# Hybrid HGRN2 / RWKV-7 / MoE trunk on one core: two branch phases joined, two gate units and 13 dense products per pair at other places

## The reference, cut to what matters

```python
xn = rmsnorm(h, norm_mix_w)
z = xn @ w_in                                   # 2048 x 11552
zq, zf, zi, zo, zs, zga, zgb = split(z)         # 4 x 1024 | 3360 | 2048 | 2048
y_hg = hgrn2_branch(zq, zf, zi, zo, lb, onorm_w)        # 8 heads of 128, chunks of 32
y_rw, _ = rwkv7_branch(zs, mu, w0, w_up, a0, a_up, g_up, ...)   # 16 heads of 64, 288 LoRA columns
merged = sigmoid(zga) * (y_hg @ w_branch_hg) + sigmoid(zgb) * (y_rw @ w_branch_rw)
h = h + merged @ w_out
h = h + hier_moe(rmsnorm(h, norm_ffn_w), ...)   # top 1 of 4 groups, top 2 of 8 experts
return rmsnorm(h, final_norm_w)
```

## Time and profile before

| | us |
|---|---|
| median of 3 runs (lowest to highest) | 3035.86 (3035.18 to 3037.81) |
| profiled execution | 3032.92 |
| its span, first to last instruction | 3031.3 |
| TensorE busy in the span | 2523.1 (83%) |
| VectorE / ScalarE / GpSimd busy | 882.5 / 825.6 / 130.6 |

### The profile page before, as it was taken

One profiled execution on the slowest core, in us unless ns is written; L12 is line 12 of the kernel. 1 busy time (PEld: TensorE's weight loads), 2 busy tenths in 40 slices (PEclk: granted clock), 3 DMA queues, 4 the chain that ended last, 5 costly groups with the idle time before them and its releaser, 6 DMA issues. The chain is left out here.

```text
span 3031.3 us, 39754 instructions
## 1 busy us (share of the span) xinstructions
PE 2523.1 (83%) x15609; PEld 1666.4 (55%) x15609; DVE 882.5 (29%) x1169; ACT 825.6 (27%) x1038; POOL 130.6 (4%) x212
## 2 busy tenths in 40 slices
PE   5999999979999999997599996587777777777770
PEld 4888888857676767676487885232222222222220
DVE  3433433324545555444344223100000000000004
ACT  4444334323433333332222222021111111111111
POOL 0000000000000000000000000200000000000000
PEclk9999999989999999997799998799999999999995
DMA  4333333332232222210544326499999999999984
GB/s 135 94 103 98 93 107 94 93 96 72 67 84 61 66 69 61 76 49 15 156 145 155 129 83 239 175 404 408 403 411 411 410 408 408 404 393 407 396 330 183
DMA packets 315386, 605.62 MB, mean 200 GB/s; under 512 B 19605, under 2 KB 243217, under 8 KB 260766
## 3 DMA queue, kind: packets, MB, share of 16 engines
q1 hardware_dynamic: 304224, 570.63, 51.7%
q0 software_dynamic: 11072, 33.64, 3.2%
HBM read 584.24 MB, written 37.78 MB: 205 GB/s over the span
## 5 line engine op out<-in xcount | busy, mean ns | idle before, releaser
L1774 PE MATMUL ex_gate_up<-ex_w_gate,ex_xt_sb 128*64 128x512 f32 x1024 | 474.9, 610 | 175.8 <-DMA ex_w_up<-in_expert_w_up_dram 172.1
L1776 PE MATMUL ex_gate_up<-ex_w_up,ex_xt_sb 128*64 128x512 f32 x1024 | 478.1, 614 | 0.0
L1774 PEld LDWEIGHTS ex_gate_up<-ex_w_gate,ex_xt_sb 128*64 128x64 f32 x1024 | 134.1, 140 | 486.6 <-issue 486.6
L150 PE MATMUL hg_z<-xn_hi,hg_hi 128*128 128x512 f32 x768 | 303.6, 395 | 13.2 <-DVE hg_lo L182 13.2
L1743 DVE TENSOR_TENSOR ex_act_g<-ex_gate_up,ex_sig 64x512 f32<-64x512 f32 x32 | 21.9, 684 | 998.3 <-ACT ex_sig L1725 998.3
L150 PE MATMUL rw_z<-xn_hi,rw_hi 128*128 128x512 f32 x688 | 290.0, 422 | 21.9 <-DVE rw_lo L182 21.9
L150 PE MATMUL hg_z<-xn_hi,hg_lo 128*128 128x512 f32 x768 | 301.3, 392 | 0.0
L150 PE MATMUL hg_z<-xn_lo,hg_hi 128*128 128x512 f32 x768 | 300.1, 391 | 0.0
L1796 PE MATMUL ex_down<-ex_w_down,ex_ht_sb 128*64 128x512 f32 x512 | 263.3, 673 | 26.1 <-ACT ex_ht_sb L1728 25.5
L150 PE MATMUL rw_z<-xn_lo,rw_hi 128*128 128x512 f32 x688 | 278.2, 404 | 0.0
L150 PE MATMUL rw_z<-xn_hi,rw_lo 128*128 128x512 f32 x688 | 272.7, 396 | 0.0
(11 more groups left out here) (373 smaller groups left out, 3570.9 us busy)
## 6 DMA issues: line engine op xcount, KB each, us to landing
ex_w_gate<-in_expert_w_gate_dram SPq DMA_DIRECT2D x128, 1024.0 KB, 16.2
ex_w_up<-in_expert_w_up_dram SPq DMA_DIRECT2D x128, 1024.0 KB, 27.8
ex_w_down<-in_expert_w_down_dram SPq DMA_DIRECT2D x128, 1024.0 KB
hg_raw<-in_w_in_dram SPq DMA_DIRECT2D x49, 1024.0 KB
rw_raw<-in_w_in_dram SPq DMA_DIRECT2D x43, 1024.0 KB
mg_raw<-in_w_out_dram SPq DMA_DIRECT2D x32, 512.0 KB
mg_raw<-in_w_branch_hg_dram SPq DMA_DIRECT2D x16, 512.0 KB
mg_raw<-in_w_branch_rw_dram SPq DMA_DIRECT2D x16, 512.0 KB
```

The source lines that it names most:

```text
L150: return pe.matmul(out, w[:, k, :], x[:, k, :], start=(n == 0), stop=(n == PASSES * KT - 1), skip_group_check=True)
L1774: pe.matmul(gate_up[low, :], x_t[u][:, k, :], w_gate[n][:, j, :], start=first, stop=last, skip_group_check=True)
L1776: mm = pe.matmul(gate_up[high, :], x_t[u][:, k, :], w_up[n][:, j, :], start=first, stop=last, skip_group_check=True)
```

## The change

1. `phase_branches` is new: one ring, one pair of PSUM tiles `z`, one pair of `z_read` semaphores and one Block for both branches. RWKV's units are numbered on from HGRN2's: BASE = 7 x 6 + 4 = 46, TURN = 23. The load that HGRN2 added at the end, only so that its last step had something to split, is now the first LoRA unit. A few RWKV tensors (`rwkv_early`) exist from the start, so that LoRA work doesn't lie over HGRN2's tensors; their constants are set by GpSimd ahead of HGRN2's. Before pair 0 ScalarE and VectorE wait for HGRN2's last gate and y stores, TensorE for its last y.
2. HGRN2's head 7 is written out and has 4 units: its two gate units go to RWKV's last pair, which now has 4 (192 products) and also the splits of units 2 and 3 and the read-outs of units 2 and 3.
3. In each RWKV pair `dense(38)` becomes `dense(45)` and `dense(6)` after the bonus sum becomes `dense(12)`. The last run shrinks by 13.
4. Every Block is opened with `no_gpsimd_drain=True`.
5. `upto`, a switch of `build`, is gone; it changes nothing that runs.

```diff
-def phase_hgrn(nc, io, keep):
+def phase_hgrn(nc, io, keep, block, sems):
-        ring = make_ring(mem, "hg")
-        z = [mem.psum(f"hg_z{b}", [P, T]) for b in range(2)]
+        ring, z, z_read = keep["ring"], keep["z"], keep["z_read"]
...
+            def head(i, last):
+                for u in range(4 if last else UNITS):
                     ring_load(sp, ring, u % 2, UNITS * i + u, w_in[:, :, bass.ds(columns(i, u), P)])
-            ring_load(sp, ring, 0, UNITS * HEADS, w_in[:, :, 0:P])
+            with sp.Fori(0, HEADS - 1) as i:
+                head(i, False)
+            head(HEADS - 1, True)
...
-                for u in range(UNITS):
+                for u in range(4 if last else UNITS):
                     if u != 2:
                         split(u + 1)
...
+                if last:
+                    square(i)
                 act.wait_ge(mean_done, i + 1)
...
+                if not last:
+                    ring_lo(dve, ring, 1, m + 5)
+                    ring_lo(dve, ring, 0, m + 6)
...
+                units = 4 if last else UNITS
-                fill(UNITS * PASSES * KT)
+                fill(units * PASSES * KT)
                 pe.wait_ge(sq_ready, i + 1)
...
-def phase_rwkv(nc, io, keep):
+def phase_rwkv(nc, io, keep, block, sems, early):
+    LAST_UNITS = 2 * HG_GATES
+    BASE = (HEADS - 1) * (4 + HG_GATES) + 4
+    TURN = BASE // 2
-        gates, g_rs = (e_neg, e_cum), ba
+        gates, g_rs = (e_neg, e_cum, cum_x, dl), ba
...
-            ring_hi(act, ring, 0, 0, 0)
-            ring_hi(act, ring, 1, 1, 0)
+            ring_hi(act, ring, 1, BASE + 1, TURN + 0)
             copy_out(0, 0, 0)
...
+            act.wait_ge(keep["hg_gate_free"], HG_GATES * HEADS)
+            act.wait_ge(keep["hg_y_free"], HEADS + 1)
...
-                if not last:
-                    split(2)
+                split(2)
...
-                    if not last and lv == 1:
+                    if lv == 1:
                         split(3)
-                    if not last and lv == 4:
+                    if lv == 4:
                         read_out(2)
-                        split(4)
+                        if not last:
+                            split(4)
...
                 if not last:
                     split(5)
-                    read_out(3)
+                read_out(3)
...
-                store_gate(0)
-                if last:
-                    store_gate(1)
+                for g in range(LAST_UNITS if last else 1):
+                    store_gate(g)
...
+            pe.wait_ge(keep["hg_y_ready"], HEADS)
-                total = PASSES * KT * (HG_GATES if last else UNITS)
+                total = PASSES * KT * (LAST_UNITS if last else UNITS)
...
-                dense(38)
+                dense(45)
...
                 pe.matmul(twin[1][:, 0, :], block64, bonus[:], start=True, stop=True).then_inc(bonus_sum, 1)
-                dense(6)
+                dense(12)
...
-        block = ctx.enter_context(nc.Block())
+        block = ctx.enter_context(nc.Block(no_gpsimd_drain=True))
...
+def phase_branches(nc, io, keep):
+    with ExitStack() as ctx:
+        mem = Memory(nc, ctx)
+        keep["ring"] = make_ring(mem, "in")
+        keep["z"] = [mem.psum(f"in_z{b}", [P, T]) for b in range(2)]
+        keep["z_read"] = mem.sem("in_z_read0", "in_z_read1")
+        early = rwkv_early(mem)
+        block = ctx.enter_context(nc.Block(no_gpsimd_drain=True))
...
+        phase_hgrn(nc, io, keep, block, mem)
+        phase_rwkv(nc, io, keep, block, mem, early)
```

More of the change, by code:

```diff
@@ L378, in _, with head @@
             pool.sem_inc(y_free, 1)
-            with pool.Fori(0, HEADS) as i:
-                for g in range(HG_GATES):
+            def head(i, last):
+                for g in range(0 if last else HG_GATES):
                     wait_apart(pool, keep["pool_waits"], z_read[g % 2], UNITS // 2 * i + 2 + g // 2 + 2)
@@ L390, in _ @@
                 pool.sem_inc(y_free, 1)
+            with pool.Fori(0, HEADS - 1) as i:
+                head(i, False)
+            head(HEADS - 1, True)
         @block.scalar
@@ L396, in _, with head @@
             act.wait_ge(const_ready, 2)
-            with act.Fori(0, HEADS) as i:
+            def head(i, last):
                 order = Order(act, act_o, ACT_STEPS * i)
@@ L447, in _, with square @@
                 assert order.n == ACT_STEPS, order.n
+            def square(i):
+                act.wait_ge(o_done, i + 1)
+                act.activation(o_sq[:], o_ps[:], ACT.Square).then_inc(sq_ready, 1)
+            with act.Fori(0, HEADS - 1) as i:
+                head(i, False)
+            head(HEADS - 1, True)
         @block.vector
@@ L456, in _, with head @@
             STEPS = 3
-            with dve.Fori(0, HEADS) as i:
+            def head(i, last):
                 order = Order(dve, dve_o, STEPS * i)
@@ L514, in _ @@
                 assert order.n == STEPS, order.n
+            with dve.Fori(0, HEADS - 1) as i:
+                head(i, False)
+            head(HEADS - 1, True)
         @block.tensor
@@ L519, in _, with head @@
             ident = keep["const"][:, CONST["ident"], :]
-            with pe.Fori(0, HEADS) as i:
+            def head(i, last):
                 m = UNITS * i
+                units = 4 if last else UNITS
                 def dense(u, n):
@@ L656, in phase_rwkv, with gate_rows @@
-        gate_stored, gate_free = mem.sem("rw_gate_stored", "rw_gate_free")
-        block = ctx.enter_context(nc.Block())
+        y_ready, y_stored, y_free = sems.sem("rw_y_ready", "rw_y_stored", "rw_y_free")
+        gate_stored, gate_free = sems.sem("rw_gate_stored", "rw_gate_free")
+        def gate_rows(p, last):
+            own = [HG_GATES * (HEADS + p) + g for g in range(HG_GATES)]
+            return own + [HG_GATES * (HEADS - 1) + g for g in range(HG_GATES)] if last else own
         @block.sync
```

189 lines of the change are left out of this document (92 added, 97 removed).

## The result

The changed kernel takes 2957.4 us as the median of 4 runs (2955.01 to 2966.88), the kernel before 3035.52 beside it (4 runs, 3032.19 to 3037.81): a ratio of 0.9749, 95% interval 0.9726 to 0.9773. The forecast was 2957.0, in a range of 2950 to 2974. The profiled execution of after is the 2966.88 one, with a span of 2965.0 us.

What follows compares the result with a forecast made beforehand. TensorE's dense products bound RWKV, by number times spacing plus stops. Gains of 45.4 + 22.4 + 0 + 11.0 = 78.8 us from 3032.92, plus 2.9 for the median, gave 2957.0 us, own range +/- 5, with A and B 2950 to 2974.

Steps and rivals of the forecast that it cites:

- Part 1, handover: HGRN2's end to RWKV's start: LoRA unit 0 read at 612.5 instead of 657.88, a gain of 45.4 us.
- Rival E: At the handover, a wait for HGRN2's stores or the first LoRA split returns up to 20 us: 2977; chance 0.04.
- Part 2: Thirteen products moved in each RWKV pair fill the waits before L1066 and L1177: 7 x 3.2 = 22.4 us gained.
- Six products fill 1.37 us. The other 0.27 us go too: At L1177, six products fill most of the 1.64 us wait; unit 3 ending some 4 us sooner removes the rest.
- It just fits: At a pair's end, ScalarE's table load ends at 1361.58, the last unit at 1361.5, so the second gate isn't delayed.
- Rival B: At the pairs' end ScalarE, held 1.28 us after a load, becomes the bound: 9.1 us less gain, 2966.1; chance 0.08.
- Part 3: In the last pair, the two moved gate units hide: cost 0 us, bounds -2 and +2.
- the balance of +1.2 and -1.2: In pair 7, a low-half split adds 1.2 us; unfilled chunks at higher clock and an omitted split save about 1.2.
- the prediction's own signs of being wrong: Idle time before a unit's first product (L150 behind lo), or pair 7 growing by more than 3 us.
- Part 4: At phase ends, GpSimd's DRAINs at L602, L1370 and L1639 vanish with the flag: 11.0 us gained.
- Rival A: At phase ends, the DRAIN's work moves to L95 or L96, a loss of 2.3 us: 2970.3; chance 0.27.
- Rivals C and D: C: 96 products don't hide in pair 7, 2978.9, chance 0.05. D: late low halves, slower than before, chance 0.01.

Runs made afterwards that it cites:

- after again: The changed kernel, unchanged, timed again with five runs beside the follow-up runs: 2958.28 us, with a second profile of 2957.2 us span.
- a_keepgates: The changed kernel with head 7's two gate units back in HGRN2 and two units in the last pair: 2975.79 us, ratio 0.9804.
- a_split2: The changed kernel with ScalarE's split of unit 2 put ahead of its read-out of unit 0 in every pair: 2950.91 us, ratio 0.9725.
- b_front7: The kernel before with dense(45) in place of dense(38) alone: 3012.17 us, one run.
- a_tload: The changed kernel with one more one-column Ln, and so one more table load, ahead of the second gate in seven pairs: 2962.61 us, ratio 0.9757.
- a_drain: The changed kernel with plain Blocks, so GpSimd's DRAINs are back: 2968.72 us, ratio 0.9778.
- b_nodrain: The kernel before with only no_gpsimd_drain=True on every Block: 3020.82 us, ratio 0.9951.

## Why the prediction was right

**Part 1, handover: right.** 45.4 said; pair 0 starts 44.5 us earlier in after and 45.4 in after again. Its parts held: 1.18 us for the Square (1.2 said), unit 0 read at 613.37 (612.5 said; all that is before it starts some 0.5 us later in after), no stretch at the lower clock, no wait for the stores. a_keepgates splits it: there pair 0 starts 24.6 us earlier than before (45.4 - 21.9 = 23.5 said), and the move of the gate units gives the other 19.9 (20.7 said: 21.9 less the 1.2 of the Square, which those products cover where they stay). Rival E did not happen.

**Part 2: the size nearly right, its reason half wrong.** 22.4 said, 24.1 measured; 3.2 us per pair against 3.4. The front seven were counted as 1.60 us and the middle six as 1.64; in truth the seven give 3.5 and the six nothing beside them. The step that failed is "Six products fill 1.37 us. The other 0.27 us go too": the reason given for the 0.27, that unit 3 ends sooner, is the reason for the whole 1.6. The sum came out because one wait was counted once, though two edits would each have removed it. Of the wait before unit 2 it said 0.4 us that cost nothing, and that holds: from the transposes to the first level 11.62 us pass before and after, the new wait and what is left of the old 0.87 standing inside them. What it didn't see is that the split behind both can come sooner, which a_split2 turns into 0.5 us a pair. The 0.2 to 0.3 us a pair beyond the forecast are won between bonus sum and mean: the view shows a wait of 1.59 there, and its going is worth 1.8 (b_front7). Nor does the chain to the operands hang at the split of unit 1 alone, as the prediction put it: 0.9 us of it were a wait for the kk sum.

"It just fits" was right for the place (the sigmoid starts 0.01 us behind its load) and too strict for the pair: a_tload delays it by a load and more and costs 0.8. Rival B, ScalarE held after a load for as long again, is in none of the rows above: the activations follow their loads at once.

**Part 3: 0 said, within 2; measured +1.0 and +1.9 in the two profiles of after, and +3.4 in a_drain's, outside the band.** That the products hide is shown by a_keepgates. The failed step is the balance of +1.2 and -1.2. Up to the first level's VectorE work (L956, L985 in after) the pair is 2.6 us longer than before instead of 1.2, over the rest of the levels and the chunks it is the same, and behind the chunks it is 0.7 us shorter in after, 1.4 in after again and 0.9 longer in a_drain. The 2.6 comes of this: the prediction took pair 6 as the picture of pair 7, but in pair 6 the read-out ahead of the split of unit 2 is a copy of 0.60 us, while in pair 7 it is the first gate, with a table load of 1.28. The term is that load: with it the last pair has 1.76 us of rest and some 1.2 of lower clock, 3.0 together by a_split2. Without it the pair takes 81.0 us, 2.0 less than before, at the end of the band on the good side; with it 84.0 to 86.4. The clock was said to stay at full until the chunk loop's end; it fell before that in all three, behind the rest of 1.8 us, and the second fall, at the end of the pair, where the spread lies, is in no term of the sum. Two of the prediction's own signs of being wrong came in part: idle time before the first product of a unit, small in seven pairs and foreseen there, 1.76 us in the last and not foreseen; and a pair 7 longer by more than 3 us, in one profile of three. The moved read-out was in the diff's new gate numbering, and I costed the new splits but not what they stand behind.

**Part 4: right.** 11.0 said for all of it. b_nodrain gives 14.8, where 13.1 was expected, since it also has the 2.0 of L322; its interval of ratios, 0.9934 to 0.9967, is 10 to 20 us. a_drain gives 11.3 of 13.0 back. Rival A, with a chance of 0.27, was not the case. The reason that the prediction gave against it, the semaphores that L95 clears, no run tests. Its price of 0.3 us for the merge's four DMAs went by their count, and the 13.6 us of that DRAIN before say that the count is not the rule there.

**The whole.** 78.8 us said, 78.1 measured between the medians. That it comes so close is in part luck: an error of +1.7 and one of the other sign nearly cancel. The shares of the errors: part 2 +1.7, part 3 -1.0 to -1.9 in the two profiles of after, the rest below what runs differ by. Rivals C and D stayed away: no wait above 1.8 us stands on TensorE in after's RWKV stage.

## What to carry to other kernels

Before filling a wait with work, follow it to its source: here a wait hung, through a split, a table load and a gate on ScalarE, at the end of a unit of TensorE's own stream, and work moved to an earlier stop dissolved it, so that filling it as well was worth nothing. When a unit of work moves to another place, list what stands in front of each of its steps there, table loads too; two exchanged lines were worth 7 us here. Count GpSimd's DMAs per phase: where it comes last to the phase's end, its DRAIN cost 82 to 88 ns for each here. In the merge the DRAIN also lasted until the transfers under way had landed, so before it is dropped, see that the kernel itself waits for every DMA before the phase ends, as this one does.

## What was not expected

- A rest of 1.76 us of TensorE in a busy stretch is followed by 3.4 us at a granted clock of 0.50 (1.2 GHz); rests of 0.3 to 0.4 us are not. With the order that makes the rest of 1.78 us changed, the pair is 3.0 us shorter.
- At the end of the last pair the clock falls at another point in each profile, and the pair's time differs by up to 2.4 us between them. What decides it stays open.
- GpSimd's DRAIN is 82 to 88 ns per DMA at 9, 24, 48 and 100 of them, all landed before, but 13.6 and 13.7 us at the merge's end with 4 under way; it ended 0.21 us behind the last landing both times.
- In the stage bound by the weight loads one profiled execution of twelve was 3 to 11 us longer than the others, with less waiting for DMA and a busier TensorE.
